# The weight sums of a seven-product stage: from VectorE to accumulating memory transfers

## The chip, the cores and the metric

The kernel runs on one core of a Trainium2 chip. The metric is the device time of one execution in microseconds (us), as the median of the runs of the same program.

## The reference

Two transformer-like blocks follow one another on a sequence of 512 tokens of width 1024, in float32. The change touches only the end of the second block, where four branches are gated and merged:

```python
branch_d = jnp.einsum('nbsw,nwd->bsnd', ys, w_branch)
g = jax.nn.sigmoid(gates.reshape(bsz, s, N_BRANCH, d))
merged = jnp.sum(g * branch_d, axis=2)
return x + merged @ w_out
```

`gates` is a product of the normalised input `h` (512 x 1024) and 4096 columns of `w_in`, so the gates are a matmul of 512 x 1024 by 1024 x 4096. `branch_d` is four products of 512 x 512 by 512 x 1024.

## The kernel before

**Splitting.** Every float32 weight is used as a sum of two reduced parts. ScalarE (ACT) copies a strip from `raw` to `w_hi` (`split_hi`, L649), VectorE (DVE) subtracts to get `w_lo` (`split_lo`, L1160), and TensorE (PE) makes three matmuls for each product: hi x hi, hi x lo, lo x hi. `w_hi` and `w_lo` have 4 places (`SPLITS`). Each engine works through the list `USED` in order; at step k, ACT and DVE make the split of step k + 3, and a split may not start before PE has finished step k - 4 of its own number (`unit_used`).

**Loading.** SP's queue loads the units of `ORDER` into `raw`, a ring of 5 strips of 512 KB (128 partitions x 1024 float32). It waits until the unit that had the place before has been split (`lo_made`).

**The seven-product stage.** The gate weights come as panels `ga`: `ga[2j]` and `ga[2j+1]` are the panels of the two branches of pair j. For pairs 2 to 15 (14 pairs) the 2 x 2 blocks of tokens and weights are multiplied by a scheme of seven instead of eight block products. The steps of one pair in `USED` are `sa`, `sb`, `br`, `sc`, `sd`: `sa` uses panel a as it is, `sb` uses two sums of weights held in the tile `s12`, `br` is the branch product, `sc` uses panel b with its left half replaced by a sum, and `sd` uses the right half of panel a after a sum has been put there. The token sums (`t_full`, `t3_full`, made by `make_tokens`) are made once, ahead of the stage. The parts are gathered in PSUM, copied and added (`gate_a`, `gate_b`), put through a sigmoid and multiplied by the branch products (`gate_pair`).

**The sums of weights before.** VectorE makes them in `combine` (L1172, L1173 for `sb`; L1176 for `sc`; L1181 for `sd`), each once per pair on 128 x 512 float32, one step before the split that needs them, and ACT's split waits for `combined`.

**GpSimd's queue.** POOL has no work between 487 us and the end of the stage: its next instruction is the reload of the kept `x2` (L620), issued when the `sb` step of the last pair has been used, and then the load of `final_row` (L623).

Of the kernel before, what the change touches and what calls it, by code (L numbers as in the profile page):

```python
# [6 lines left out]
P = 128  # L7
# [9 lines left out]
RING = 5  # L17
SPLITS = 4
AHEAD = SPLITS - 1
# [30 lines left out]
UNIT = {u: n for n, u in enumerate(ORDER)}  # L50
# [3 lines left out]
FIRST_PAIR, LAST_PAIR = 2, 2 * KT - 1  # L54
USED = []
# [5 lines left out]
HALF = S // 2  # L61
# [12 lines left out]
STEP = {u: k for k, u in enumerate(USED)}  # L74
# [158 lines left out]
def program(nc, dram, out):  # L233
    f32, f32r, bf16, i32 = mybir.dt.float32, mybir.dt.float32r, mybir.dt.bfloat16, mybir.dt.int32
    ALU, ACT, AX = mybir.AluOpType, mybir.ActivationFunctionType, mybir.AxisListType
    with ExitStack() as ctx:
# [163 lines left out]
        def sem(name):  # L400
            return ctx.enter_context(nc.semaphore(name))
# [35 lines left out]
        tiles_made, f_heads_made = sem("tiles_made"), sem("f_heads_made")  # L437

        x2_saved, x2_here = sem("x2_saved"), sem("x2_here")
        t_step, t_hi_made, combined = sem("t_step"), sem("t_hi_made"), sem("combined")  # L440
        part_made, part_kept, part_added = sem("part_made"), sem("part_kept"), sem("part_added")
        sig_made, gated = sem("sig_made"), sem("gated")
        x2_rstd, x2_norm_made, x2T_made, h2_hi_made, h2_made = (
# [44 lines left out]
        def raw_of(unit):  # L488
            return raw[:, UNIT[unit] % RING, :]
# [14 lines left out]
        def banks_of(p):  # L504

            return side if p % 2 == 0 else acc
# [50 lines left out]
        def _(pool):  # L557
# [54 lines left out]
            for t in range(1, TT):  # L612
                pool.wait_ge(relu_used, 4 * t)
                diagonal = score[:, t - 1, t * P:(t + 1) * P]
                nc.gpsimd.affine_select(out=diagonal, in_=diagonal, compare_op=ALU.is_ge, fill=OUTSIDE, base=0,
                                        pattern=[[-1, P]], channel_multiplier=1).then_inc(cut_made, 1)
            pool.wait_ge(unit_used, STEP["sb", LAST_PAIR] + 1)
            pool.wait_ge(x2_saved, 16)
            for half in (slice(0, S), slice(S, D)):
# [6 lines left out]
        def _(act):  # L626
# [8 lines left out]
            def split_hi(k):  # L635

                kind, j = USED[k]
                if kind == "sb":
                    act.wait_ge(combined, 3 * (j - FIRST_PAIR) + 1)
                elif kind == "sc":  # L640
                    act.wait_ge(combined, 3 * (j - FIRST_PAIR) + 2)
                elif kind == "sd":
                    act.wait_ge(combined, 3 * (j - FIRST_PAIR) + 3)
                else:
                    n = UNIT["ga", 2 * j] if kind == "sa" else UNIT[kind, j]
                    act.wait_ge(raw_in[n % RING], 16 * (n // RING + 1))
                if k >= SPLITS and (kind, j) != ("bs", 0):
                    act.wait_ge(unit_used, k - SPLITS + 1)
                nc.scalar.activation(split_at(k)[0][:, 0:WIDTH.get(kind, U)], strip_of(k), ACT.Copy).then_inc(hi_made, 1)  # L649
# [199 lines left out]
            for k, (kind, j) in enumerate(USED):  # L849
# [159 lines left out]
                if (kind, j) in (("dq", 2), ("dq", 3)):  # L1009
                    n = j - 1  # L1010
# [19 lines left out]
                    nc.scalar.activation(gate_b[:, :], banks_of(j)[0][:, 0:HALF], ACT.Copy).then_inc(part_kept, 1)  # L1030
                if kind == "sc":
                    act.wait_ge(gated, 2 * p)
                    nc.scalar.activation(sig[:, 1, 0:HALF], banks_of(j)[0][:, 0:HALF], ACT.Sigmoid).then_inc(sig_made, 1)
                    act.wait_ge(part_added, 3 * p + 2)
                    nc.scalar.activation(sig[:, 1, HALF:], gate_b[:, :], ACT.Sigmoid).then_inc(sig_made, 1)
                if kind == "sd":
                    act.wait_ge(part_added, 3 * p + 1)
                    act.wait_ge(part_added, 3 * p + 3)
# [29 lines left out]
        def _(dve):  # L1068
            done = [0]

            def then(ins):

                done[0] += 1
                ins.then_inc(dve_chain, 1)
                dve.wait_ge(dve_chain, done[0])
# [84 lines left out]
                nc.vector.tensor_tensor(out=lo[:, 0:width], in0=strip_of(k), in1=hi[:, 0:width].bitcast(f32),  # L1160
                                        op=ALU.subtract).then_inc(lo_made, 1)

            def combine(k):

                kind, j = USED[k] if k < len(USED) else (None, 0)
                if kind not in ("sb", "sc", "sd"):
                    return
                a, b, n = raw_of(("ga", 2 * j)), raw_of(("ga", 2 * j + 1)), j - FIRST_PAIR + 1
                if kind == "sb":
                    for u in (("ga", 2 * j), ("ga", 2 * j + 1)):  # L1170
                        dve.wait_ge(raw_in[UNIT[u] % RING], 16 * (UNIT[u] // RING + 1))
                    then(nc.vector.tensor_tensor(out=s12[:, 0, :], in0=b[:, 0:512], in1=b[:, 512:1024], op=ALU.add))  # L1172
                    nc.vector.tensor_tensor(out=s12[:, 1, :], in0=s12[:, 0, :], in1=a[:, 0:512], op=ALU.subtract)\  # L1173
                        .then_inc(combined, 1)
                if kind == "sc":
                    nc.vector.tensor_tensor(out=b[:, 0:512], in0=a[:, 0:512], in1=b[:, 0:512], op=ALU.subtract)\  # L1176
                        .then_inc(combined, 1)
                if kind == "sd":
                    dve.wait_ge(combined, 3 * (n - 1) + 1)
                    dve.wait_ge(lo_made, STEP["sa", j] + 1)  # L1180
                    nc.vector.tensor_tensor(out=a[:, 512:1024], in0=a[:, 512:1024], in1=s12[:, 1, :], op=ALU.subtract)\  # L1181
                        .then_inc(combined, 1)

            def difference(dst, part, hi, lo, hi_less, lo_less):

                then(nc.vector.tensor_tensor(out=dst, in0=hi, in1=hi_less, op=ALU.subtract))
                then(nc.vector.tensor_tensor(out=part, in0=lo, in1=lo_less, op=ALU.subtract))
                nc.vector.tensor_tensor(out=dst, in0=dst, in1=part, op=ALU.add).then_inc(t_step, 1)

            def make_tokens(kind, j):  # L1190

                hi = {(r, c): quarter(hT_hi, r, c).bitcast(f32) for r in (0, 1) for c in (0, 1)}
                lo = {(r, c): quarter(hT_lo, r, c).bitcast(f32) for r in (0, 1) for c in (0, 1)}
                full, rest = {n: t[:, :, :] for n, t in t_full.items()}, {n: t[:, :, :] for n, t in t_rest.items()}
                if (kind, j) == ("dq", 1):
                    dve.wait_ge(x2_saved, 16)
                    difference(full[1], rest[1], hi[0, 1], lo[0, 1], hi[0, 0], lo[0, 0])
                if (kind, j) == ("dq", 2):
                    dve.wait_ge(t_step, T_STEP[1, "full"])
                    then(nc.vector.tensor_tensor(out=full[2], in0=hi[1, 1], in1=full[1], op=ALU.subtract))  # L1200
                    nc.vector.tensor_tensor(out=full[2], in0=full[2], in1=lo[1, 1], op=ALU.add).then_inc(t_step, 1)
                if (kind, j) in (("dq", 3), ("dk", 0)):
                    n = 1 if kind == "dq" else 2
                    dve.wait_ge(t_step, T_STEP[2, "full"])
                    dve.wait_ge(t_hi_made, n)
                    nc.vector.tensor_tensor(out=t_lo[n][:, :, :], in0=full[n], in1=t_hi[n][:, :, :].bitcast(f32),
                                            op=ALU.subtract).then_inc(t_step, 1)
                if (kind, j) == ("ga", 1):
                    difference(t3_full[:, :, :], t3_part[:, :, :], hi[1, 1], lo[1, 1], hi[0, 1], lo[0, 1])
                if (kind, j) == ("ga", 2):  # L1210
                    dve.wait_ge(t_step, T_STEP[2, "lo"])
                    difference(full[4], rest[4], hi[1, 0], lo[1, 0],
                               t_hi[2][:, :, :].bitcast(f32), t_lo[2][:, :, :].bitcast(f32))
                if (kind, j) == ("ga", 3):
                    dve.wait_ge(t_step, T_STEP[4, "full"])
                    dve.wait_ge(t_hi_made, 3)
                    nc.vector.tensor_tensor(out=t_lo[4][:, :, :], in0=full[4], in1=t_hi[4][:, :, :].bitcast(f32),
                                            op=ALU.subtract).then_inc(t_step, 1)
                if (kind, j) == ("br", 1):
                    dve.wait_ge(t_step, T_STEP[3, "full"])  # L1220
                    dve.wait_ge(t_hi_made, 4)
                    nc.vector.tensor_tensor(out=quarter(hT_lo, 0, 1), in0=t3_full[:, :, :],
                                            in1=quarter(hT_hi, 0, 1).bitcast(f32), op=ALU.subtract).then_inc(t_step, 1)
# [303 lines left out]
            for k, (kind, j) in enumerate(USED):  # L1527
                if k + 1 < KT:
                    modulate(k + 1)
                    if k + 2 < KT:  # L1530
                        if k:
                            sum_modulation(k + 2, 0)
                        sum_modulation(k + 2, 1)
                    lower_h(k + 1)
                    for later_k in to_split(k):
                        split_lo(later_k)
                elif (kind, j) not in (("wo", 14), ("wo", 15)):
                    combine(k + AHEAD + 1)
                    for later_k in to_split(k):
                        split_lo(later_k)  # L1540
                n = HEAD_AT.get((kind, j))
# [862 lines left out]
```

## Time and profile before

| | |
|---|---|
| median of 3 runs | 1111.63 us (1111.48 to 1111.64) |
| span of the profiled execution | 1109.4 us |
| PE busy | 1100.7 us, 99% |
| DVE busy | 744.2 us, 67% |
| ACT busy | 506.9 us, 46% |
| POOL busy | 19.8 us, 2% |

The span runs from the first to the last instruction of one profiled execution. That execution has no device time of its own on record; the median of the three runs is 2.2 us above its span. Busy shares are averages over stages with different limits, and a matmul's end is modelled, so a busy PE is read by the distance between matmul starts rather than by the share.

### The profile page before, as it was taken

To read this page: it belongs to the slowest core of one execution; us is meant where nothing else is said; L and a number is where in the kernel's file an instruction comes from. 1 tells how busy PE (TensorE), PEld (TensorE's weight loads), DVE (VectorE), ACT (ScalarE), POOL (GpSimd) and SP (SyncE) were. 2 spreads that over 40 slices of the span, in tenths; PEclk is the share of its full clock that TensorE was granted. 3 is DMA by queue.
4 is the path that set the end of the run, shared out by engine and by line. 5 is a ranking of instruction groups with operands and counts; after the bars stand their busy time and mean duration, and the time that the engine had idled before them with its cause. 6 is when DMAs were issued, how large, how long until landed. Compare 5 with 4: busy or idle time off the path is not lost.

```text
span 1109.4 us, 18066 instructions
## 1 busy us (share of the span) xinstructions
PE 1100.7 (99%) x7344; PEld 931.1 (84%) x7344; DVE 744.2 (67%) x1195; ACT 506.9 (46%) x851; POOL 19.8 (2%) x40
## 2 busy tenths in 40 slices
PE   9999999999999999999999999999999999999997
PEld 8888888888888888878888887887789999999986
DVE  6875876864686247448789896447568677667853
ACT  7562354324675225533342434336544444444543
POOL 1000000000001001000000000000000000000000
PEclk9999999999999999999999999999999999999999
DMA  9543324432215433522223232231121322333241
GB/s 372 220 149 125 125 68 133 127 102 73 74 58 167 139 95 111 185 74 79 77 76 95 77 95 68 66 114 58 58 73 61 114 93 80 115 115 114 81 186 76
DMA packets 33618, 121.09 MB, mean 109 GB/s; under 512 B 3824, under 2 KB 3824, under 8 KB 33536
## 3 DMA queue, kind: packets, MB, share of 16 engines
q1 hardware_dynamic: 30672, 109.88, 29.7%
q0 software_dynamic: 2720, 10.03, 2.7%
q8 instruction: 58, 0.95, 0.4%
q14 instruction: 24, 0.20, 0.1%
q10 hardware_dynamic: 144, 0.03, 0.0%
HBM read 115.74 MB, written 4.19 MB: 108 GB/s over the span
## 4 chain that ended last, share of the span: by engine, by line
PE 98%; DMA 1%; DVE 1%; ACT 0%; SPq 0%; issue 0%; ACTq 0%
PE acc L1829 22%; PE acc L1831 21%; PE acc L1830 21%; PE acc L1841 2%; PE side L1841 2%; PE acc L1839 2%; PE side L1839 2%; PE acc L1837 2%; PE side L1837 2%; PE acc L2189 2%; PE side L1829 2%; PE side L1830 2%; PE side L1831 2%; PE side L2071 2%; PE side L1984 2%; PE side L2189 1%
## 5 line engine op out<-in xcount | busy, mean ns | idle before, releaser
L1160 DVE TENSOR_TENSOR w_lo<-raw,w_hi 128x1024 fp32r<-128x1024 f32 (+2 forms) x194 | 225.8, 1165 | 149.7 <-ACT w_hi L649 146.8
L1829 PE MATMUL acc<-hT_hi,w_hi 128*128 128x512 f32 x648 | 258.9, 400 | 0.0
L1831 PE MATMUL acc<-hT_hi,w_lo 128*128 128x512 f32 x648 | 252.8, 390 | 0.0
L1830 PE MATMUL acc<-hT_lo,w_hi 128*128 128x512 f32 x648 | 252.4, 390 | 0.0
L649 ACT ACTIVATE w_hi<-raw 128x1024 fp32r<-128x1024 f32 (+2 forms) x194 | 195.6, 1009 | 115.4 <-PE acc L1831 87.7
L1829 PEld LDWEIGHTS acc<-hT_hi,w_hi 128*128 128x128 f32 x648 | 121.9, 188 | 26.9 <-issue 2.9
L1831 PEld LDWEIGHTS acc<-hT_hi,w_lo 128*128 128x128 f32 x648 | 121.6, 188 | 26.1
L1830 PEld LDWEIGHTS acc<-hT_lo,w_hi 128*128 128x128 f32 x648 | 121.9, 188 | 23.6
L1829 PE MATMUL acc<-w_hi,hT_hi 128*128 128x512 f32 (+1 forms) x152 | 60.3, 396 | 0.0
L1831 PE MATMUL acc<-w_hi,hT_lo 128*128 128x512 f32 (+1 forms) x152 | 58.8, 387 | 0.0
L1830 PE MATMUL acc<-w_lo,hT_hi 128*128 128x512 f32 (+1 forms) x152 | 58.7, 386 | 0.0
L1160 DVE TENSOR_TENSOR w_lo<-s,w_hi 128x1024 fp32r<-128x1024 f32 x14 | 17.2, 1225 | 39.8 <-ACT w_hi L649 39.8
L912 ACT ACTIVATE silu_e<-acc 128x512 f32<-128x512 f32 x32 | 19.0, 594 | 53.8 <-PE acc L1831 53.8
L1829 PEld LDWEIGHTS acc<-w_hi,hT_hi 128*128 128x128 f32 x152 | 28.5, 188 | 6.3 <-issue 1.0
L1831 PEld LDWEIGHTS acc<-w_hi,hT_lo 128*128 128x128 f32 x152 | 28.5, 188 | 5.6
L1830 PEld LDWEIGHTS acc<-w_lo,hT_hi 128*128 128x128 f32 x152 | 28.6, 188 | 5.4 <-issue 0.2
L789 ACT ACTIVATE probs<-side,small 128x128 f32<-128x128 f32 (+3 forms) x32 | 16.9, 529 | 34.3 <-DVE small L1448 25.1
L1841 PE MATMUL side<-hT_hi,w_lo 128*128 128x256 f32 x112 | 31.7, 283 | 0.0
L1841 PE MATMUL acc<-hT_hi,w_lo 128*128 128x256 f32 x112 | 31.7, 283 | 0.0
L1839 PE MATMUL side<-hT_lo,w_hi 128*128 128x256 f32 x112 | 31.7, 283 | 0.0
L1839 PE MATMUL acc<-hT_lo,w_hi 128*128 128x256 f32 x112 | 31.7, 283 | 0.0
L1837 PE MATMUL acc<-hT_hi,w_hi 128*128 128x256 f32 x112 | 31.7, 283 | 0.0
(461 smaller groups left out, 2251.5 us busy)
## 6 DMA issues: line engine op xcount, KB each, us to landing
raw<-in_ga SPq DMA_DIRECT2D x32, 512.0 KB, 4.5
ada_raw<-in_ada SPq DMA_DIRECT2D x16, 512.0 KB, 11.5
raw<-in_wo SPq DMA_DIRECT2D x16, 512.0 KB, 3.5
raw<-in_br SPq DMA_DIRECT2D x16, 512.0 KB, 3.5
raw<-in_q SPq DMA_DIRECT2D x8, 512.0 KB, 3.5
raw<-in_u SPq DMA_DIRECT2D x8, 512.0 KB, 4.0
raw<-in_gp SPq DMA_DIRECT2D x8, 512.0 KB, 4.5
raw<-in_ada_w SPq DMA_DIRECT2D x8, 512.0 KB, 3.6
```

The costliest lines, as they stand in the source:

```text
L649: nc.scalar.activation(split_at(k)[0][:, 0:WIDTH.get(kind, U)], strip_of(k), ACT.Copy).then_inc(hi_made, 1)
L912: nc.scalar.activation(gate_e(gates), acc[RESULT[kind, j] % 4][:, :], ACT.Exp, scale=-1.0)\
L1160: nc.vector.tensor_tensor(out=lo[:, 0:width], in0=strip_of(k), in1=hi[:, 0:width].bitcast(f32), op=ALU.subtract).then_inc(lo_made, 1)
L1829: nc.tensor.matmul(ps, w[0], x[0], start=first, stop=False)
L1830: nc.tensor.matmul(ps, w[0], x[1], start=False, stop=False)
L1831: return nc.tensor.matmul(ps, w[1], x[0], start=False, stop=last)
L1837: nc.tensor.matmul(out_, w[0][:, cols], x[0][:, kt, :], start=first and kt == 0, stop=False, skip_group_check=not first)
L1839: nc.tensor.matmul(out_, w[0][:, cols], x[1][:, kt, :], start=False, stop=False, skip_group_check=not first)
L1841: ins = nc.tensor.matmul(out_, w[1][:, cols], x[0][:, kt, :], start=False, stop=kt == 3, skip_group_check=not first)
L1984: ins = nc.tensor.matmul(ps[p0:p0 + B, n0:n0 + width], k[:, tok], right, start=True, stop=True)
L2071: ins = nc.tensor.matmul(side[3][:, h * P:(h + 1) * P], v, probsT[:, s % 2, b * P:(b + 1) * P], start=(b == 0), stop=(b == blocks - 1))
L2189: return nc.tensor.matmul((acc + side)[h][:, :], w[:, h * P:(h + 1) * P], x[:, j, :], start=start and j == 0, stop=stop and j == KT - 1)
```

## The change

The four VectorE sums of each pair go. In their place POOL's queue issues five DMA transfers for each pair, four of which accumulate (they add to what the destination holds): the first puts the left half of b into both halves of `s12`, the second adds the right half of b to both, the third adds the left half of a to the left half of b in `raw`, the fourth adds the left half of a to the second half of `s12`, and the fifth adds the second half of `s12` to the right half of a in `raw`. ACT's splits wait for the transfers' semaphores. The transfers only add, so the scheme is one with only plus signs among the weights: the token sums change sign accordingly, and the sigmoids of the second gate read their input with scale -1.

```diff
+            pool.wait_ge(t_step, T_STEP[3, "full"])
+            for j in range(FIRST_PAIR, LAST_PAIR + 1):
+                ga, summed_here = dram["ga"], 64 * (j - FIRST_PAIR)
+                a, b = raw_of(("ga", 2 * j)), raw_of(("ga", 2 * j + 1))
+                twice = [ga[2 * j + 1, :, n:n + 512].unsqueeze(1).broadcast_to([P, 2, 512]) for n in (0, 512)]
+                if j > FIRST_PAIR:
+                    pool.wait_ge(lo_made, STEP["sb", j - 1] + 1)
+                    pool.wait_ge(s12_sum, summed_here)
+                pool.dma_start(s12[:, :, :], twice[0]).then_inc(s12_sum, 16)
+                pool.wait_ge(s12_sum, summed_here + 16)
+                pool.dma_start(s12[:, :, :], twice[1], accum_op=ALU.add).then_inc(s12_sum, 16)
+                n = UNIT["ga", 2 * j + 1]
+                pool.wait_ge(raw_in[n % RING], 16 * (n // RING + 1))
+                if j > FIRST_PAIR:
+                    pool.wait_ge(b_sum, 16 * (j - FIRST_PAIR))
+                pool.dma_start(b[:, 0:512], ga[2 * j, :, 0:512], accum_op=ALU.add).then_inc(b_sum, 16)
+                pool.wait_ge(s12_sum, summed_here + 32)
+                pool.dma_start(s12[:, 1, :], ga[2 * j, :, 0:512], accum_op=ALU.add).then_inc(s12_sum, 16)
+                pool.wait_ge(s12_sum, summed_here + 48)
+                pool.wait_ge(lo_made, STEP["sa", j] + 1)
+                pool.dma_start(a[:, 512:1024], s12[:, 1, :], accum_op=ALU.add).then_inc(s12_sum, 16)
             pool.wait_ge(unit_used, STEP["sb", LAST_PAIR] + 1)
...
                 if kind == "sb":
-                    act.wait_ge(combined, 3 * (j - FIRST_PAIR) + 1)
+                    act.wait_ge(s12_sum, 64 * (j - FIRST_PAIR) + 48)
                 elif kind == "sc":
-                    act.wait_ge(combined, 3 * (j - FIRST_PAIR) + 2)
+                    act.wait_ge(b_sum, 16 * (j - FIRST_PAIR) + 16)
                 elif kind == "sd":
-                    act.wait_ge(combined, 3 * (j - FIRST_PAIR) + 3)
+                    act.wait_ge(s12_sum, 64 * (j - FIRST_PAIR) + 64)
...
-                    nc.scalar.activation(sig[:, 1, 0:HALF], banks_of(j)[0][:, 0:HALF], ACT.Sigmoid).then_inc(sig_made, 1)
+                    nc.scalar.activation(sig[:, 1, 0:HALF], banks_of(j)[0][:, 0:HALF], ACT.Sigmoid, scale=-1.0).then_inc(sig_made, 1)
                     act.wait_ge(part_added, 3 * p + 2)
-                    nc.scalar.activation(sig[:, 1, HALF:], gate_b[:, :], ACT.Sigmoid).then_inc(sig_made, 1)
+                    nc.scalar.activation(sig[:, 1, HALF:], gate_b[:, :], ACT.Sigmoid, scale=-1.0).then_inc(sig_made, 1)
...
-            def combine(k):
...
-                if kind == "sb":
-                    for u in (("ga", 2 * j), ("ga", 2 * j + 1)):
-                        dve.wait_ge(raw_in[UNIT[u] % RING], 16 * (UNIT[u] // RING + 1))
-                    then(nc.vector.tensor_tensor(out=s12[:, 0, :], in0=b[:, 0:512], in1=b[:, 512:1024], op=ALU.add))
-                    nc.vector.tensor_tensor(out=s12[:, 1, :], in0=s12[:, 0, :], in1=a[:, 0:512], op=ALU.subtract)\
-                        .then_inc(combined, 1)
-                if kind == "sc":
-                    nc.vector.tensor_tensor(out=b[:, 0:512], in0=a[:, 0:512], in1=b[:, 0:512], op=ALU.subtract)\
-                        .then_inc(combined, 1)
-                if kind == "sd":
-                    dve.wait_ge(combined, 3 * (n - 1) + 1)
-                    dve.wait_ge(lo_made, STEP["sa", j] + 1)
-                    nc.vector.tensor_tensor(out=a[:, 512:1024], in0=a[:, 512:1024], in1=s12[:, 1, :], op=ALU.subtract)\
-                        .then_inc(combined, 1)
...
-                    combine(k + AHEAD + 1)
```

In `make_tokens` the first difference swaps its operands, and the second and fourth token sums get one `scalar_tensor_tensor` each (with the factor -1) in place of a `tensor_tensor`; the number of instructions stays the same.

## Rows read from the trace of the kernel before

**Rows 1.** Stages: us, each engine's busy time, granted PE clock, DMA share, GB/s.
```profile
core 0: us, PE busy (x) PEld busy (x) DVE busy (x) ACT busy (x) POOL busy (x), PEclk, DMA share, GB/s
...
857.10:1042.00 184.90, 184.90 (x1283) 173.11 (x1283) 133.93 (x185) 80.84 (x130) 0.00 (x0) 1.00 0.29 102
...
1100.00:1109.40 9.40, 3.45 (x16) 2.52 (x14) 3.45 (x5) 4.67 (x12) 0.00 (x0) 0.93 0.55 223
```

**Rows 2.** Lines L1837 and L1172: durations min/median/max, first and last start.
```profile
L1837 PE MATMUL acc<-t_hi,w_hi x84: 277/283/283, 860.0 to 1057.6; 128*128 128x256 f32 x84
...
L1172 DVE TENSOR_TENSOR s<-raw x14: 679/682/693, 831.4 to 1035.7; 128x512 f32<-128x512 f32 x14
```

**Rows 3.** Timeline of one pair: start us, duration us, engine, line, operation [idle before].
```profile
917.88 1.23 DVE L1160 TENSOR_TENSOR w_lo<-s,w_hi 128x1024 fp32r<-128x1024 f32 x1 [3.06 <-ACT w_hi L649]
...
932.09 0.28 PE L1837 MATMUL acc<-t_hi,w_hi 128*128 128x256 f32 x1
932.21 0.28 PE L1839 MATMUL acc<-t_lo,w_hi 128*128 128x256 f32 x1
...
932.35 1.06 ACT L649 ACTIVATE w_hi<-s 128x1024 fp32r<-128x1024 f32 x1 [2.42 <-PE side L1831]
...
933.45 1.23 DVE L1160 TENSOR_TENSOR w_lo<-s,w_hi 128x1024 fp32r<-128x1024 f32 x1 [3.06 <-ACT w_hi L649]
...
937.85 0.28 PE L1837 MATMUL side<-t_hi,w_hi 128*128 128x256 f32 x1
```

**Rows 4.** The same pair, branch matmuls: two successive starts.
```profile
931.64 0.39 PE L1830 MATMUL side<-yd_lo,w_hi 128*128 128x512 f32 x1
931.87 0.39 PE L1831 MATMUL side<-yd_hi,w_lo 128*128 128x512 f32 x1
```

**Rows 5.** DVE's timeline after the split of `s12`, same pair.
```profile
934.59 0.69 DVE L1176 TENSOR_TENSOR raw<-raw 128x512 f32<-128x512 f32 x1
935.40 1.23 DVE L1160 TENSOR_TENSOR w_lo<-raw,w_hi 128x1024 fp32r<-128x1024 f32 x1
936.54 0.42 DVE L1241 TENSOR_TENSOR gate_a<-acc,gate_a 128x256 f32<-128x256 f32 x1
936.88 0.68 DVE L1248 TENSOR_TENSOR merged_part<-side,sig 128x512 f32<-128x512 f32 x1
937.59 0.69 DVE L1252 TENSOR_TENSOR m_full<-m_full,merged_part 128x512 f32<-128x512 f32 x1
938.32 0.69 DVE L1248 TENSOR_TENSOR merged_part<-acc,sig 128x512 f32<-128x512 f32 x1
```

**Rows 6.** DMA issues by tile: count, KB each, median us from issue to landing.
```profile
raw<-in_wo SPq DMA_DIRECT2D x16, 512.0 KB, 3.5
...
x_kept<-x POOLq DMA_DIRECT2D x1, 2048.0 KB, 8.5
...
raw<-in_pw SPq DMA_DIRECT2D x4, 256.0 KB, 2.6
...
gate_row<-in_gate_b POOLq DMA_DIRECT2D x1, 512.0 KB, 4.4
...
final_row<-in_final_g POOLq DMA_DIRECT2D x1, 512.0 KB, 7.4
...
kv_row<-in_kv_g POOLq DMA_DIRECT2D x1, 64.0 KB, 5.6
```

**Rows 7.** DMA queues over the span: packets, MB, share of 16 engines.
```profile
q1 hardware_dynamic: 30672, 109.88, 29.7%
q0 software_dynamic: 2720, 10.03, 2.7%
```

**Rows 8.** DMA issues in one pair, 925.7 to 941.4 us.
```profile
raw<-in_ga SPq DMA_DIRECT2D x2, 512.0 KB, 6.3
raw<-in_br SPq DMA_DIRECT2D x1, 512.0 KB, 4.3
```

**Rows 9.** Timeline of the start and the end of the stage, DVE and ACT.
```profile
826.98 1.23 DVE L1188 TENSOR_TENSOR t_full<-t_full,t_part 128x1024 f32<-128x1024 f32 x1
...
832.88 1.06 ACT L649 ACTIVATE w_hi<-s 128x1024 fp32r<-128x1024 f32 x1 [1.35 <-DVE s L1173]
...
1041.27 1.06 ACT L649 ACTIVATE w_hi<-s 128x1024 fp32r<-128x1024 f32 x1 [2.42 <-PE side L1831]
```

**Rows 10.** POOL's queue: issues of DMAs, and the wait before them.
```profile
338.05 0.56 POOL L593 DMA_DIRECT2D gate_row<-in_gate_b  x1 [233.12 <-PE acc L1831]
...
1050.11 1.53 POOL L620 DMA_DIRECT2D x<-x_kept  x2 [562.73 <-PE acc L1841]
```

More of the change, by code:

```diff
@@ L439, in program @@
         x2_saved, x2_here = sem("x2_saved"), sem("x2_here")
-        t_step, t_hi_made, combined = sem("t_step"), sem("t_hi_made"), sem("combined")
+        t_step, t_hi_made = sem("t_step"), sem("t_hi_made")
+        s12_sum, b_sum = sem("s12_sum"), sem("b_sum")
         part_made, part_kept, part_added = sem("part_made"), sem("part_kept"), sem("part_added")
@@ L1161, in split_lo @@
                                         op=ALU.subtract).then_inc(lo_made, 1)
-            def combine(k):
[L1165 to L1168, printed above, removed]
-                if kind == "sb":
-                    for u in (("ga", 2 * j), ("ga", 2 * j + 1)):
-                        dve.wait_ge(raw_in[UNIT[u] % RING], 16 * (UNIT[u] // RING + 1))
-                    then(nc.vector.tensor_tensor(out=s12[:, 0, :], in0=b[:, 0:512], in1=b[:, 512:1024], op=ALU.add))
-                    nc.vector.tensor_tensor(out=s12[:, 1, :], in0=s12[:, 0, :], in1=a[:, 0:512], op=ALU.subtract)\
-                        .then_inc(combined, 1)
-                if kind == "sc":
-                    nc.vector.tensor_tensor(out=b[:, 0:512], in0=a[:, 0:512], in1=b[:, 0:512], op=ALU.subtract)\
-                        .then_inc(combined, 1)
-                if kind == "sd":
-                    dve.wait_ge(combined, 3 * (n - 1) + 1)
-                    dve.wait_ge(lo_made, STEP["sa", j] + 1)
-                    nc.vector.tensor_tensor(out=a[:, 512:1024], in0=a[:, 512:1024], in1=s12[:, 1, :], op=ALU.subtract)\
-                        .then_inc(combined, 1)
             def difference(dst, part, hi, lo, hi_less, lo_less):
@@ L1196, in make_tokens @@
                     dve.wait_ge(x2_saved, 16)
-                    difference(full[1], rest[1], hi[0, 1], lo[0, 1], hi[0, 0], lo[0, 0])
+                    difference(full[1], rest[1], hi[0, 0], lo[0, 0], hi[0, 1], lo[0, 1])
                 if (kind, j) == ("dq", 2):
                     dve.wait_ge(t_step, T_STEP[1, "full"])
-                    then(nc.vector.tensor_tensor(out=full[2], in0=hi[1, 1], in1=full[1], op=ALU.subtract))
-                    nc.vector.tensor_tensor(out=full[2], in0=full[2], in1=lo[1, 1], op=ALU.add).then_inc(t_step, 1)
+                    then(nc.vector.scalar_tensor_tensor(out=full[2], in0=hi[1, 1], scalar=-1.0, in1=full[1],
+                                                        op0=ALU.mult, op1=ALU.subtract))
+                    nc.vector.tensor_tensor(out=full[2], in0=full[2], in1=lo[1, 1], op=ALU.subtract).then_inc(t_step, 1)
                 if (kind, j) in (("dq", 3), ("dk", 0)):
@@ L1211, in make_tokens @@
                     dve.wait_ge(t_step, T_STEP[2, "lo"])
-                    difference(full[4], rest[4], hi[1, 0], lo[1, 0],
-                               t_hi[2][:, :, :].bitcast(f32), t_lo[2][:, :, :].bitcast(f32))
+                    then(nc.vector.tensor_tensor(out=full[4], in0=hi[1, 0], in1=t_hi[2][:, :, :].bitcast(f32), op=ALU.add))
+                    then(nc.vector.tensor_tensor(out=rest[4], in0=lo[1, 0], in1=t_lo[2][:, :, :].bitcast(f32), op=ALU.add))
+                    nc.vector.scalar_tensor_tensor(out=full[4], in0=full[4], scalar=-1.0, in1=rest[4],
+                                                   op0=ALU.mult, op1=ALU.subtract).then_inc(t_step, 1)
                 if (kind, j) == ("ga", 3):
```

## The prediction

> **What bounds the kernel now.** I read the page's engine table first: PE is busy 99% of the span, so something must make PE wait, or must make its work shorter, before the time moves. The change leaves the matmuls as they are. Then I read the stages. In the seven-product stage PE shows no idle time, at full granted clock, while DVE is busy 133.9 of 184.9 us and the DMA engines 29% [rows 1]. The sums recur 14 times between 831.4 and 1035.7 us, so a pair takes 204.3 / 13 = 15.7 us [rows 2]. PE's own work for a pair is 84 matmuls of 256 columns, which start 0.12 us apart [rows 3], and 24 of 512 columns, 0.23 us apart [rows 4]: 10.1 + 5.5 = 15.6 us. So PE is the bound of a pair to within 0.1 us, and all that DVE, ACT and the DMAs do must fit into 15.7 us.
>
> Next I read one pair's timeline for the slack of the step that gets its weights latest from the sums, `sb`. ACT may split `s12` at 932.35, when PE has ended `br` of the pair before; DVE's part ends at 933.45 + 1.23 = 934.68; PE starts `sb` at 937.85 [rows 3]. The slack is 3.2 us.
>
> **What is taken away.** Four DVE sums per pair of 0.69 us, 2.8 us of DVE time [rows 2, 5]. DVE is not the bound, and PE has 0.1 us to recover in a pair, so this is worth at most 14 x 0.1 = 1.4 us, and I count it as 0. ACT's waits for these sums go too, but PE has never waited for them. The token sums keep their number and size; the sign of the sigmoid's scale is a parameter of the same instruction: 0.
>
> **What is added.** Five transfers per pair on POOL's queue. I call them D1 to D5 in order of issue. POOL waits for D1 before it issues D2, for D2 before D4, for D4 before D5, and before the next D1 for D5 and for the split of `s12` (`lo_made` of `sb`). That is a ring: the four transfers D1, D2, D4, D5 follow one another, each from issue to landing, and the next pair can't start them earlier since there is one `s12`. No double buffer lets two pairs overlap. D3 is issued while D2 runs and has `b_sum` of its own; it is needed only two steps later. SP's queue and its waits are unchanged, and behind the waiting instructions on POOL stand only the reload of `x2` and `final_row`, which wait for PE's last `sb` anyway [rows 10]. Behind ACT's wait for D4 stand the sigmoids of the pair before and the split of the next `br`, behind these DVE's gating, and for the gating PE's next `br` waits.
>
> The budgets, from the rows of before: from the end of the split of one `s12` (917.88 + 1.23 = 919.11) to the start of ACT's split of the next (932.35) are 13.2 us, and 16.4 us with the slack [rows 3]. D1 + D2 + D4 have to fit in there. And D1 + D2 + D4 + D5 have to fit in 15.7 us, or the ring gets longer than PE's pair and every pair pays the difference.
>
> **The price of one transfer.** The trace has no accumulating DMA and no DMA from POOL in this stage. Rates first: 30672 packets of queue 1 carried 109.88 MB in 29.7% of 16 x 1109.4 us, or 20.8 GB/s for each engine, 333 GB/s for all; queue 0, POOL's, comes to the same [rows 7]. So 512 KB take 1.6 us and 256 KB 0.8 us of moving. POOL's lightly loaded transfers then leave a fixed part: `gate_row` 4.4 - 1.6 = 2.8 us; the store of 2048 KB 8.5 - 6.3 = 2.2 us [rows 6]. I take 2.5. SP's queue is shorter, 3.5 us for 512 KB and 2.6 for 256 KB [rows 6]; these are the lower bound. POOL's under load were 7.4 us for 512 KB and 5.6 for 64 KB [rows 6]; these are the upper bound for a plain one.
>
> An accumulating transfer must also read its destination. From below this costs nothing more, if that read runs beside the other; from above I allow that it doubles the whole transfer, fixed part included, if destination reads are not overlapped. I take the middle that follows from the rate: the bytes that are read count twice.
>
> - D1, 512 KB, plain: 2.5 + 1.6 = 4.1 us.
> - D2, 512 KB, accumulating: 2.5 + 3.1 = 5.6 us, and 0.8 us because D3's 256 KB go through the same engines at that time: 6.4.
> - D4 and D5, 256 KB, accumulating: 2.5 + 1.6 = 4.1 us each.
> - POOL's wake-up and issue between them, 0.1 us each: 0.4 us. An issue itself keeps POOL 0.56 us, which lies in the landing times [rows 10].
> - SP's three loads of 512 KB per pair come in one burst, and in this stage they take 4.3 and 6.3 us against 3.5 alone [rows 6, 8]. One or another member of the ring meets this burst: 0.8 us.
>
> The ring: 4.1 + 6.4 + 4.1 + 4.1 + 0.4 + 0.8 = 19.9 us, say 20.0, against 15.7. Below, with nothing for accumulating and nothing for company: 4.1 + 4.1 + 3.3 + 3.3 + 0.4 = 15.2, and 12.2 with SP's durations. Above: 4.1 + 8.2 + 6.6 + 6.6 + 2.0 = 27.5.
>
> **The sum.** D1 of the first pair waits for the third token sum, which ends at 826.98 + 1.23 = 828.2 [rows 9]. D4 lands 4.1 + 6.4 + 4.1 + 0.3 = 14.9 us later, at 843.1, ten us after ACT's first split of `s12` before (832.88). PE notices only part of that. D4 of the last pair lands 13 rings later, 843.1 + 260 = 1103.1. Before, this split started at 1041.3 and could have started 3.2 us later without PE's noticing, at 1044.5 [rows 3, 9]. The delay at PE is 58.6 us. Add the gating: after the split of `s12` starts, DVE needs until 938.32 + 0.69 - 933.45 = 5.6 us from the start of its own part to end the second product, less the removed sum (0.7), so 1.1 + 4.9 = 6.0 us after ACT's start [rows 3, 5]; I allow 0.4 for ACT's share of it. PE, which starts `sb` 2.3 us after ACT's start and needs 24 x 0.12 = 2.9, wants to begin `br` 5.2 us after it: 1.2 us more for the last pair. For the others this lies within the ring's surplus. After the last pair all is as before, since SP's loads for the last product and the reload of `x2` shift along. Together 60 us. The span would be 1109.4 + 60 = 1169.4 us, and with the 2.2 us by which the median stands above the span, 1171.6: I say 1172 us.
>
> In each pair PE then stands still for about 20.0 - 15.6 = 4.4 us, in one or two pieces, before `sb` and before `br`.
>
> **Rivals.**
>
> *The transfers stay hidden (no change).* What decides is the point at which D1 + D2 + D4 + D5 with their gaps pass 15.7 us. If accumulating costs nothing and the fixed part is as small as SP's, the ring is 12.2 us; with POOL's fixed part and nothing else 15.2. Either gives PE its weights in time, as D1 + D2 + D4 are then 9.6 or 11.8 us against 13.2. The time would be 1111.6, less up to 1.4 us for PE's last tenth. For it speaks that rates on both queues are alike [rows 7]; against it speak the slower rows of POOL's queue, the company of D3 and of SP's burst (with these 1.6 us the ring is 16.8 and the time 1128), and that the destination has to be read. The Trainium skill's page "DMA: Bandwidth & Descriptors", section "Anatomy of one DMA — SWDGE (gpsimd) path", gives a transfer from this queue as about 2.0 us plus its bytes at 436 GB/s; an estimate from that page is 3.2 + 3.2 + 2.6 + 2.6 = 11.6 us, and by it the change would cost nothing. The trace disagrees with it so far as `gate_row` goes, 4.4 us against 3.2. Chance of this rival: 0.12, of which 0.02 fall to a gain above 0.2%.
>
> *Accumulating is much slower than moving.* At twice the whole duration the ring is 27.5 us, D4 of the last pair lands at 828.2 + 20.0 + 357.5 = 1205.7, the delay is 162 us, and the time 1274. No row speaks against it, as none accumulates. Chance 0.13 for a ring beyond 24 us.
>
> *TensorE's clock falls in the pauses.* In the stage it is granted in full; at the end of the kernel, where PE works 3.45 of 9.4 us, the mean is 0.93 [rows 1]. Were half of each pair's matmuls to run at 1.2 GHz, PE's pair would take 15.6 + 7.8 = 23.4 us plus the 1.2 of gating, which passes the ring by 4.6 us: 13 x 4.6 = 60 us more, 1232. Pauses of some 4 us are short and much of the slowing would use up surplus of the ring. Chance 0.08.
>
> *My forecast,* a ring of 16 to 24 us with the clock kept: 0.67. Its own range is 16.8 us (1128) to 24 us: 828.2 + 18 + 13 x 24 = 1158, less 1044.5, plus 1.2, or 1226.
>
> **The range.** From the forecast's own 1128 to 1226 (0.67), down to take in the edge where the ring barely passes the pair, up to the clock's case and the lighter part of slow accumulation: 1118 to 1255. Left out are about 0.11 below and 0.08 above.
>
> **Chances.** A measurement of this kernel tells some 0.2% (2.2 us) from no change. Faster 0.02, within 0.2% 0.10, slower 0.88.
>
> **What would show each step.** In the profile after: POOL's issues of D1 recur every 20 us instead of PE's 15.7, with D5's landing as the releaser, not DVE's `lo_made`. ACT's split of `s12` waits for a DMA and not for PE. PE has an idle piece before the matmuls on `t_hi` in each pair, released by `w_lo`. D1's landing is near 4.1 us, D2's 6, D4's and D5's 4. DVE's busy time is 14 x 2.8 = 39 us less. The forecast is wrong if the durations of the accumulating transfers lie outside these, if the start shows that pairs can run ahead of one another, or if PE's clock in the stage is under 1.00.

## The result, and the profile after

The changed kernel takes 1204.49 us (median of 3 runs, 1204.13 to 1205.54) against 1111.63: ratio 1.0838, 95% interval 1.0818 to 1.0857. It is slower by 92.9 us; 60 were forecast. The profiled execution has a span of 1203.8 us, 94.4 more than before. Of all executions quoted here one stands apart and is in no median: the fourth of experiment 3 took 1364.06 us at a mean granted clock of 0.753, the other three 1140 to 1142 us at 0.994 to 0.995.

The page of the kernel after: engines (busy us, share of the span, instructions), and from its list of groups the two that name the loss (busy us, mean ns, then idle time before them and its releaser).

```profile
PE 1130.3 (94%) x7342; PEld 952.0 (79%) x7344; DVE 710.6 (59%) x1139; ACT 503.6 (42%) x851; POOL 83.5 (7%) x110
...
L671 ACT ACTIVATE w_hi<-s 128x1024 fp32r<-128x1024 f32 x14 | 14.8, 1056 | 125.7 <-DMA s<-in_ga 125.7
...
L1840 PE MATMUL acc<-t_hi,w_hi 128*128 128x256 f32 x84 | 30.8, 367 | 31.4 <-DVE w_lo L1182 21.6
```

ACT's split of `s12` now waits for a transfer in each of the 14 pairs, where in 13 of them it waited for PE before [rows 3, 9]. And PE waits, at the first matmul of `sb`. Its waits in the stage, by line (total us, times, longest), from the weight loads that stand ahead of the matmuls:

```profile
PEld acc L1840 <- DVE w_lo L1182: 23.0, 7, 4.4
PEld side L1840 <- DVE w_lo L1182: 20.9, 8, 5.2
PEld side L1840 <- ACT gate_a L1045: 14.6, 7, 2.3
PEld acc L1840 <- ACT gate_a L1045: 11.8, 7, 2.3
```

Before, PE waited for nobody in the stage. The first two rows are the wait for the split of `s12`, 43.9 us or 3.1 in the mean of the 14 pairs. The last two are a second pause within `sb`, 26.4 us or 1.9 in the mean, up to 2.3: the second half of `sb` goes into a bank that ACT must have copied (`gate_a`), and ACT gets to that copy only after two more splits and three sigmoids.

One ring on POOL's queue (start, time of the issue, idle before it and releaser). L626 is D1, L628 D2, L633 D3, L635 D4, L638 D5:

```profile
935.86 0.75 POOL L626 DMA_DIRECT2D s<-in_ga  x1 [3.00 <-DVE w_lo L1182]
940.26 1.19 POOL L628 DMA_DIRECT2D s<-in_ga  x1 [3.65 <-DMA s<-in_ga]
941.00 1.36 POOL L633 DMA_DIRECT2D raw<-in_ga  x1
950.12 0.84 POOL L635 DMA_DIRECT2D s<-in_ga  x1 [7.76 <-DMA s<-in_ga]
954.36 0.84 POOL L638 DMA_DIRECT2D raw<-s  x1 [3.40 <-DMA s<-in_ga]
958.19 0.75 POOL L626 DMA_DIRECT2D s<-in_ga  x1 [2.99 <-DVE w_lo L1182]
```

From D1 to D1 are 22.3 us: 4.4 to D2, 9.9 to D4, 4.2 to D5, 3.8 to the next D1. The label of the last row calls `w_lo` the releaser, but that split (below) had ended at 956.42; D5, issued at 954.36 and landed 3.3 us later, at 957.7, came last.

The durations from issue to landing over all 14 pairs (min, median, max), D1, D2, D4 and D5 in this order:

```profile
DMA to landing us min/median/max: 3.9/4.1/4.1
...
DMA to landing us min/median/max: 5.8/9.5/10.3
...
DMA to landing us min/median/max: 4.0/4.0/7.6
...
DMA to landing us min/median/max: 3.3/3.3/3.3
```

D2 is the long one, and its spread says that it is not long by nature: the first pair's took 5.8. What else runs in that ring is on SP's, ACT's, DVE's and PE's timelines:

```profile
940.81 0.33 SPq L549 DMA_DIRECT2D raw<-in_br  x1
941.18 0.91 SPq L549 DMA_DIRECT2D raw<-in_ga  x2
...
954.10 1.06 ACT L671 ACTIVATE w_hi<-s 128x1024 fp32r<-128x1024 f32 x1 [9.86 <-DMA s<-in_ga]
...
955.19 1.23 DVE L1182 TENSOR_TENSOR w_lo<-s,w_hi 128x1024 fp32r<-128x1024 f32 x1 [10.49 <-ACT w_hi L671]
...
956.47 0.39 PE L1840 MATMUL acc<-t_hi,w_hi 128*128 128x256 f32 x1 [4.15 <-DVE w_lo L1182]
...
957.47 0.41 PE L1840 MATMUL acc<-t_hi,w_hi 128*128 128x256 f32 x1
957.68 0.41 PE L1842 MATMUL acc<-t_lo,w_hi 128*128 128x256 f32 x1
...
960.28 0.58 PE L1840 MATMUL acc<-t_hi,w_hi 128*128 128x256 f32 x1 [1.33 <-ACT gate_a L1045]
```

SP's three loads of 512 KB are issued 0.6 to 1.8 us after D2. From the third ring on the first of them comes between 0.4 us before and 0.7 us after D2's issue, since these loads too wait for the last pair's splits. In the second ring it came 3.3 us after D2, and there D4 took the 7.6 us and D2 only 6.0. In the pair shown, the matmuls of `sb` start 0.21 us apart from 956.9 us on, and not 0.12 as before [rows 3]. Over the stage the DMA engines are busy 62%, and PE's clock is no longer granted in full (PE, PEld, DVE, ACT, POOL busy, clock, DMA share, GB/s):

```profile
842.00:1120.00 278.00, 217.20 (x1337) 197.47 (x1336) 113.80 (x146) 86.06 (x140) 56.10 (x62) 0.90 0.62 150
```

### The profile page after: what moved, and what is told of

The parts are those of the page before. It is cut to its first block, busy times and chain, and to the rows that moved or that the text cites. A ratio compares the mean times of both kernels' runs of the same rounds, so it can differ in the third digit from the quotient of the medians.

```text
span 1203.8 us, 18098 instructions
## 1 busy us (share of the span) xinstructions
PE 1130.3 (94%) x7342; PEld 952.0 (79%) x7344; DVE 710.6 (59%) x1139; ACT 503.6 (42%) x851; POOL 83.5 (7%) x110
## 4 chain that ended last, share of the span: by engine, by line
PE 73%; issue 13%; DMA 6%; POOL 3%; ACT 2%; DVE 2%; SPq 0%; POOLq 0%; ACTq 0%; DVEq 0%
PE acc L1832 19%; PE acc L1834 18%; PE acc L1833 18%; DMA s<-in_ga 5%; PE acc L2192 2%; PE side L2074 1%; PE side L1987 1%; PE side L2192 1%; DVE w_lo L1182 1%; POOL s L628 1%; ACT w_hi L671 1%; POOL raw L633 1%; PE side L2059 1%; PE side L1833 1%; PE side L1832 1%
## 5 line engine op out<-in xcount | busy, mean ns | idle before, releaser
L671 ACT ACTIVATE w_hi<-s 128x1024 fp32r<-128x1024 f32 x14 | 14.8, 1056 | 125.7 <-DMA s<-in_ga 125.7
L1840 PE MATMUL acc<-t_hi,w_hi 128*128 128x256 f32 x84 | 30.8, 367 | 31.4 <-DVE w_lo L1182 21.6
L1840 PE MATMUL side<-t_hi,w_hi 128*128 128x256 f32 x84 | 26.3, 313 | 32.3 <-DVE w_lo L1182 19.2
L1840 PEld LDWEIGHTS acc<-t_hi,w_hi 128*128 128x128 f32 x84 | 20.8, 248 | 35.1 <-DVE w_lo L1182 23.0
L1840 PEld LDWEIGHTS side<-t_hi,w_hi 128*128 128x128 f32 x84 | 17.0, 202 | 35.5 <-DVE w_lo L1182 20.6
L626 POOL DMA_DIRECT2D s<-in_ga x14 | 10.4, 744 | 380.7 <-DVE t_full L1189 341.2
```

The lines of the kernel that those rows point to most:

```text
L1840: nc.tensor.matmul(out_, w[0][:, cols], x[0][:, kt, :], start=first and kt == 0, stop=False, skip_group_check=not first)
```

## The experiments

Eleven kernels ran, each timed in several rounds beside the kernel before. All are edits of the changed kernel, except the one without sums, which is an edit of the kernel before. The rings quoted are the mean distance of D1's issues, first to last, over 13.

**1. No burst.** SP's loads from pair 3 on are cut short.

```diff
                 width = WIDTH.get(kind, U)
+                if kind == "ga" and j >= 2 * FIRST_PAIR + 2 or kind == "br" and j > FIRST_PAIR:
+                    width, src = 16, src[:, 0:16]
```

> SP's loads of the gate panels and branch strips from pair 3 on bring 16 columns in place of 1024, so the weights used there are stale; all waits and all of POOL's transfers stay. Theory A (the second transfer of the ring is long because SP's burst of three loads of 512 KB shares the DMA engines with it): its landing time falls from 9.5 us to that of the first pair, 5.8 to 6.4, the ring from 22.3 to about 19 us, the time from 1204 to about 1160 us. Theory B (accumulating from HBM is slow by itself): 9.5 us stays, and 1204 us. Theory C (the third transfer, issued beside the second, takes its share): most of the 9.5 us stays, the time falls by under 15 us.

Measured: 1161.68 us, ratio 1.0455 (1.0436 to 1.0474). Landings of D1, D2 and D4:

```profile
DMA to landing us min/median/max: 3.8/4.1/4.3
...
DMA to landing us min/median/max: 5.5/6.0/7.3
...
DMA to landing us min/median/max: 3.9/4.0/5.3
```

Only D2 is shorter, 6.0 in place of 9.5. The ring is 19.0 and not 22.2 us, and 13 x 3.2 = 41 us are what the time fell by (42.8). So the burst makes D2 long; that accumulating from HBM takes 9.5 us by itself is refuted.

**2. D3 late.** The block that issues D3 is moved behind the wait for D4.

```diff
                 pool.dma_start(s12[:, :, :], twice[1], accum_op=ALU.add).then_inc(s12_sum, 16)
+                pool.wait_ge(s12_sum, summed_here + 32)
+                pool.dma_start(s12[:, 1, :], ga[2 * j, :, 0:512], accum_op=ALU.add).then_inc(s12_sum, 16)
+                pool.wait_ge(s12_sum, summed_here + 48)
...
                 pool.dma_start(b[:, 0:512], ga[2 * j, :, 0:512], accum_op=ALU.add).then_inc(b_sum, 16)
-                pool.wait_ge(s12_sum, summed_here + 32)
-                pool.dma_start(s12[:, 1, :], ga[2 * j, :, 0:512], accum_op=ALU.add).then_inc(s12_sum, 16)
-                pool.wait_ge(s12_sum, summed_here + 48)
```

> The third transfer (256 KB into panel b) is issued after the fourth has landed, just ahead of the fifth, no more beside the second. Theory A (SP's burst makes the second long): it stays above 8 us; some 0.8 to 1.5 us less, the ring near 21.5 plus what the third takes from the fifth and first, so the time between 1190 and 1210 us. Theory C (the third transfer makes it long): the second falls to about 6 us, the ring to 19, the time to about 1165 us, unless the third lengthens the fifth and first by as much.

Measured: 1218.12 us, ratio 1.0956 (1.0940 to 1.0973), slower than the change itself and 8 us above the upper end of what was expected. Landings of D2 and D5:

```profile
DMA to landing us min/median/max: 5.6/8.3/9.0
...
DMA to landing us min/median/max: 4.7/4.8/6.2
```

D2 gains 1.2 us and D5 loses 1.5, since now D3 goes beside it. The 1.2 us are not the price of D3's company alone, for the burst has moved as well: its first load now comes 1.2 to 1.6 us before D2 in most pairs, where it came some 0.5 us after it. Without a burst D3 costs D2 little: the first pair has none in either kernel, and D2 takes 5.6 us here and 5.8 with D3 beside it. POOL must also issue D3 (0.55 us to the next issue) between D4 and D5, where before this lay under D2. The ring is 23.1. As a time, D3 had stood in the cheaper place.

**3. Plain copies.** The four accumulating transfers lose `accum_op=ALU.add`; D2's line is shown, and D3, D4 and D5 change likewise.

```diff
-                pool.dma_start(s12[:, :, :], twice[1], accum_op=ALU.add).then_inc(s12_sum, 16)
+                pool.dma_start(s12[:, :, :], twice[1]).then_inc(s12_sum, 16)
...
```

> All five transfers of a pair are plain copies of the same sizes, none accumulates, so the sums of weights are not made. If the read of the destination is a real load (my sum counted it as bytes read twice: 1.6 us in the second, 0.8 in the fourth and fifth), the ring falls by about 3 us or more, since the third also moves less: 1155 to 1170 us. Theory B (accumulating is slow by itself): the second falls from 9.5 to about 4.5 us, the ring to about 16, and the time to 1120 to 1130 us. If accumulating costs nothing: 1204 us as after.

Measured: 1141.57 us, ratio 1.0267 (1.0249 to 1.0284); ring 17.4 us. The time lies between the two ranges expected, and so confirms neither. Landings of D1, D2, D4 and D5:

```profile
DMA to landing us min/median/max: 3.9/4.0/4.5
...
DMA to landing us min/median/max: 3.8/4.0/6.3
...
DMA to landing us min/median/max: 2.9/5.8/6.4
...
DMA to landing us min/median/max: 2.3/2.3/4.8
```

Here the fastest ones are free of company. Against the fastest accumulating ones, adding costs D2 1.6 to 1.8 us (5.6 with D3 out of the way, 5.8 with it, against 4.0), D4 1.1 (4.0 against 2.9) and D5 1.0 (3.3 against 2.3). The burst has moved: it starts 1.2 to 1.7 us after D2 in most pairs and meets D4, whose median is 2.9 us above its fastest. The ring is shorter by 4.8 us; 1.7 + 1.1 + 1.0 = 3.8 of it is the three additions, the rest less company.

**4. Burst late.** SP's loads of a pair's two panels wait for D4 of the pair before; the load of the branch strip is not held back.

```diff
                 width = WIDTH.get(kind, U)
+                if kind == "ga" and j % 2 == 0 and j // 2 >= FIRST_PAIR + 2:
+                    sp.wait_ge(s12_sum, 64 * (j // 2 - 1 - FIRST_PAIR) + 48)
```

> SP's loads of the gate panels of pair j wait in addition for the fourth transfer of pair j - 1, so that the burst no longer meets the second transfer but the fifth and the first. Theory A (whatever transfer of the ring meets the burst gets longer by 3 to 4 us): the second falls to about 6 us, the fifth or first grow, and the time changes little, 1185 to 1215 us. Rival (it is the second alone that suffers, because it moves most bytes and has the third beside it): the ring falls to 19 to 20 us and the time to 1165 to 1180 us.

Measured: 1207.14 us, ratio 1.0860 (1.0840 to 1.0881). Landings of D2 and D5:

```profile
DMA to landing us min/median/max: 5.5/5.7/8.3
...
DMA to landing us min/median/max: 3.3/6.8/7.0
```

D2 gives back 3.8 us and D5 takes 3.5 more; the ring, 22.2 us, is what it was, and the time can't be told from the change's (1.0818 to 1.0857). So the long duration goes with the burst and does not belong to D2. The branch strip's load alone, some 1.2 us behind D1, leaves D1's median at 4.1 us; in two pairs D1 takes 5.5 and 6.1.

**5. Two tiles for the sums.** Odd pairs up to 11 use two places of `m_full` that are not in use yet, and D1 of the next pair is issued beside D4 of this one; semaphores are split accordingly.

```diff
+        s12b = at("s12b", M + 12288, [P, 2, 4 * P])
+
+        def s12_of(j):
+            return s12b if j % 2 and j <= 11 else s12
...
+                pool.dma_start(s_j[:, 1, :], ga[2 * j, :, 0:512], accum_op=ALU.add).then_inc(d45, 16)
+                early = j < LAST_PAIR and s12_of(j + 1) is not s_j
+                if early:
+                    copy_b(j + 1)
+                pool.wait_ge(d45, 32 * p + 16)
```

> Odd pairs up to 11 keep their sums in a second tile of 4 KB per partition (two places of m_full that are not yet in use), and the first transfer of the next pair is issued beside the fourth of this one. For pairs 2 to 12 the ring is then the second and the longer of fourth and first: 9.8 + 4.4 = 14.2 us, under PE's 15.6. Theory D (the time is set by the chain of waits, one transfer after another, and not by how much the DMA engines move): those pairs run at PE's pace, only pairs 13 to 15 pay 6 to 7 us each and the start some: 1130 to 1145 us. Rival E (the engines' load, 0.62 of their time in the stage, sets it): the transfers only get longer, 1185 us or more.

Measured: 1141.72 us, ratio 1.0271 (1.0254 to 1.0288). The middle of the stage:

```profile
860.00:1020.00 160.00, 156.04 (x1078) 145.43 (x1077) 88.45 (x115) 66.90 (x109) 42.89 (x47) 1.00 0.85 210
```

With the same transfers, now 85% of the DMA engines' time and 210 GB/s, PE is busy 156 of 160 us at full clock. The load on the engines is higher than in the changed kernel, and the loss is gone where two pairs overlap. So the chain of waits sets the time, not the load. Of the 30 us that are left, pairs 13 to 15, which have one tile and rings of 22.4 us, would account for some 20 (an estimate, 3 x 6.7).

**6. Two tiles up to pair 5.** The same with `j <= 5`: six rings of four transfers more.

> The kernel with two tiles for the sums, but the second is used only by pairs 3 and 5, so that the pairs from 7 on have the ring of four transfers; 6 more rings than in the run up to pair 11, which took 1141.7 us. If the loss is a fixed 22.4 - 15.6 = 6.8 us for each ring: 1141.7 + 6 x 6.8 = 1182 us, within 4. If the loss is due to the load on the DMA engines as a whole, it does not follow the number of rings: under 1165 or over 1195 us.

Measured: 1184.25 us, ratio 1.0650 (1.0634 to 1.0666). Six rings cost 42.5 us, 7.1 each, where 22.4 - 15.6 = 6.8 was expected.

**7. Only two sums by transfers.** DVE makes the two sums of `s12` again (all plus signs); D3 and D5 stay with POOL, and D1, D2 and D4 go.

```diff
+                then(nc.vector.tensor_tensor(out=s12[:, 0, :], in0=b[:, 0:512], in1=b[:, 512:1024], op=ALU.add))
+                nc.vector.tensor_tensor(out=s12[:, 1, :], in0=s12[:, 0, :], in1=a[:, 0:512], op=ALU.add)\
+                    .then_inc(s_made, 1)
```

> VectorE makes the two sums of s12 again; only the sum in panel b (third transfer) and that in panel a (fifth) are made by accumulating transfers, so no ring is left: VectorE's sums start from the loaded panels. Theory D (the chain of four dependent transfers is the whole loss): the two that remain, 4 and 3.3 us beside other traffic, are hidden, 1110.5 to 1113 us, as before; VectorE's relief of 1.4 us per pair gains nothing that can be measured. Rival (what costs is accumulating beside the splits, or POOL's issues): part of the 93 us remains, over 1120 us.

Measured: 1111.01 us, ratio 0.9995 (0.9987 to 1.0004): no change that can be told. D3 and D5 take 7.0 and 7.3 us (medians) in the company of each other and the burst, and are hidden.

**8. No sums at all,** in the kernel before: the four sums of each pair are left out, and the split of `s12` reads panel b.

```diff
...
-                    combine(k + AHEAD + 1)
...
```

> The kernel before with the four sums of each pair left out altogether, not made by anybody; ACT's splits wait for the loads instead. It is the most that relieving VectorE could give. My sum put this at 0 to 1.4 us (0.1 us of each pair's 15.7): 1110.2 to 1111.6 us. Rival (VectorE's load holds PE back somewhere in the stage): 1106 us or less.

Measured: 1111.29 us, ratio 0.9997 (0.9988 to 1.0006). Freeing DVE of all four sums is worth nothing that can be measured. Experiments 7 and 8 bound the gain that the change could have had; no version tried beats the kernel before by more than the measurement tells.

**9. Filler matmuls.** 32 matmuls of 256 columns whose result is overwritten, ahead of the wait in `sb`, in pairs 3 to 15.

```diff
                 if kind == "sb":
+                    if p:
+                        for n in range(FILL):
+                            nc.tensor.matmul(ps[2][:, 0:HALF], h[0, 0][0][:, 0, 0:P], h[0, 0][0][:, 0, :],
+                                             start=True, stop=True)
                     w = weights(k)
```

> As after, and 32 matmuls of 128 x 256 into the bank half that the step overwrites are put ahead of the wait for the split of s12 in pairs 3 to 15: 3.8 us of work in PE's pause of some 3 to 4 us, so that PE is hardly idle there. Theory D (the ring sets the pace and PE's clock falls within its surplus): the same within 3 us, 1201 to 1208 us, and the granted clock in the stage rises from 0.90 to 0.97 or more. Rival (the fallen clock costs some us in each pair): 1190 us or less.

Measured: 1194.17 us, ratio 1.0748 (1.0732 to 1.0765). Neither theory's figure: 10 us less than the change, with the clock in the stage at 0.98. Landings of D1 and D2:

```profile
DMA to landing us min/median/max: 3.5/3.7/3.9
...
DMA to landing us min/median/max: 5.6/8.7/10.1
```

The gain is in the transfers: the ring is 21.4 us, 13 x 0.85 = 11 us less in all. It isn't PE's own work that got faster and let the kernel end earlier, for the ring holds no PE work. What shortens D2 goes with the burst's timing. Where its first load comes 1.0 to 1.1 us after D2 (pairs 5, 6 and 13), D2 takes 7.7 to 7.9 us; where it comes 0.4 us after (pairs 8 and 10), 9.4 to 9.6. That the one causes the other is not tested by itself.

**10. Ten fillers** in place of 32.

> As the kernel with filler matmuls, but 10 in place of 32, 1.2 us of work, which leaves PE a pause of 2 to 3 us before the split of s12 arrives. If the gain of 10 us goes with the share of time in which PE is busy: 1199 to 1202 us. If it goes with the clock being kept or not: near 1194 us where the granted clock in the stage is 0.97 or more, near 1204 us where it is 0.90.

Measured: 1202.81 us, ratio 1.0815 (1.0789 to 1.0841), ring 22.0, D1 3.9 and D2 9.2 us, clock 0.94 in the stage. Ring, D1, D2 and clock all lie between the kernels with no filler and with 32, but the time can't be told from the change's (1.0818 to 1.0857).

**11. Fillers without the burst.**

> The kernel with 32 filler matmuls ahead of the wait for the split of s12, and at once SP's loads from pair 3 on cut to 16 columns (stale weights). Filler alone gave 1194.2 us, against 1204.5; its first transfer landed in 3.7 us and not 4.1, its second in 8.7 and not 9.5, and the burst came 0.4 to 0.5 us later against the second. If the filler's gain is a matter of when the burst comes, nothing is left of it without a burst: 1161 us, as the run without burst alone, first transfer 4.1. If busy matmuls make the transfers themselves shorter: first transfer 3.7, ring 18.6 or less, 1150 to 1156 us.

Measured: 1164.87 us, ratio 1.0478 (1.0460 to 1.0495). D1 is 3.8 us (4.1 without fillers) but the ring 18.9, 0.1 less than in experiment 1. As a time this run is inconclusive: with a ring of 19 us the fillers, 3.8 us on top of 15.6, no longer fit into PE's pause, and PE becomes the bound: it waits only 3.3 us in the whole stage, and from the last D4's issue to the end are 78.1 us, against 71.3 in experiment 1. The ring itself never waited for PE: each D1 follows D5's landing as closely as before. So it says that nearly all of the filler's 0.85 us needs the burst; the filler shifts SP's loads 0.3 to 0.4 us against D2. Why D1 lands 0.3 to 0.4 us sooner stays open, and the fillers may not be the cause: in this run the first pair's D1, ahead of any filler, took 3.7 us already.

## Why the prediction was right, and where it was off

**What bounds the kernel, and what the change could gain: right.** PE was the bound, DVE's relief was counted as 0, and experiment 8 gives the same. DVE's busy time fell by 33.6 us instead of 39, because neighbouring DVE instructions overlap by some 0.1 us and busy time counts the overlap once.

**The ring: right, and shown.** Four transfers in a chain, longer than PE's pair, each pair paying the difference. Experiment 5 removes the loss by letting two pairs overlap, with all transfers kept; experiment 6 puts the price back in proportion. The rival of hidden transfers fell: the smallest ring seen with one tile, that of plain copies, is 17.4 us, over 15.7.

**The start: right, to the tenth by luck.** D4 of the first pair was to land at 843.1; it was issued at 839.13 and took 4.0, which is 843.1. D1 was issued at 828.67 and not 828.2, and the gaps were longer by 0.3 us in all; D2, free of the burst, took 5.8 and not 6.4.

**The step that was off is the price of company in the ring's sum:** 0.8 us for D3 and 0.8 us for SP's burst, 1.6 together. Measured they are 3.9 together: D2's median is 9.5 us, against 5.6 in the one pair with neither D3 nor burst beside it (experiment 2, first pair). The burst makes nearly all of it: 3.5 us go when it is taken away (9.5 - 6.0, experiment 1), and D3 without a burst makes some 0.2 to 0.4 (5.8 to 6.0 against 5.6), half of its term or less. The burst's 1.6 MB need 4.7 us at 333 GB/s, and it seems that D2 has to share with most of it. I had read the price from how much SP's loads are lengthened by each other and thought of a chance meeting [rows 8]; but the burst is released by splits that follow from the ring's own D4, so it meets a member of the ring every time, and experiment 4 shows that shifting it only chooses the victim. The other terms, forecast and measured: D1 4.1 and 4.1; D2 alone 5.6 and 5.6; D4 4.1 and 4.0; D5 4.1 and 3.3; the gaps 0.4 and 1.4, taken from the distances of the issues (22.3) less the four landings (20.9); they are three of 0.3 and, ahead of D1, one of 0.54. The errors partly cancel: company 2.3 and gaps 1.0 too little, D5 0.8 and D4 0.1 too much, 2.4 in all. So the ring was 20.0 in the forecast and is 22.45 on the mean from the first D4 to the last (839.13 to 1130.92, over 13): 13 x 2.45 = 32 us, and 60 + 32 = 92 us of 94.4. The rest comes behind the last ring: from the landing of the last D4 to the end are 68.9 us (1134.9 to 1203.8), where the sum had 66.3.

**The cost of adding: near in size.** That the bytes read count twice was an assumption, 1.6 us for 512 KB and 0.8 for 256; measured 1.6 to 1.8 and 1.0 to 1.1 (experiment 3). Two sizes don't show that the second read is what costs the time.

**The pauses of PE: near in sum, and wrong in the second's cause.** 4.4 us were forecast for each pair, all of the ring's surplus. Measured are 5.0 in the mean (3.1 + 1.9), of a surplus of 22.4 - 15.7 = 6.7. The remaining 1.7 go, as far as the pair shown tells, into matmuls at the lower clock: some 20 of them start 0.09 us later each than before, about 2 us. For the second I had named DVE's gating ahead of `br`; it is the bank that ACT has yet to copy, ACT being late with all that stands behind its wait for D4.

**The clock: wrong, and cheap.** It was to be kept; it is 0.90 in the stage. The first matmuls after the two pauses shown take 0.39 and 0.58 us against 0.28. That the clock's fall is nearly free was argued with the ring's surplus, and holds as far as the runs go: with it kept at 0.98 (experiment 9) the gain of 10 us is matched by that of the rings, 11.

**The prediction's own signs.** It named three signs of being wrong, and two of them are met: D2 takes 9.5 us and not about 6, and the clock in the stage is under 1.00. The third is not: no pair ran ahead of another. The time of 1204 us lies within 1118 to 1255, with the main mechanism right and a term of it mis-sized.

## What to carry to other kernels

Before work is handed from an engine to DMA, count the dependent transfers of one round, each from issue to landing, and compare the sum with the round of the bounding engine: here 22 us (20 forecast) against 15.7, though the DMA engines were only 62% busy, and for the sake of 2.8 us of an engine whose work lay beside the path. A loop of transfers through one buffer is a latency chain, and here a second buffer broke it, where cheaper transfers (plain ones, ring 17.4 us) did not. Where a burst of other loads is released by the same event as the chain, put most of its moving time on the chain: here 3.5 us of 4.7, where 0.8 had been allowed.

## What the runs showed of the hardware

- An accumulating transfer costs 1.6 to 1.8 us more than a plain one at 512 KB (5.6 to 5.8 against 4.0 us) and 1.0 to 1.1 more at 256 KB (3.3 against 2.3 from SBUF, 4.0 against 2.9 from HBM). Plain ones on POOL's queue mostly land in 3.8 to 4.1 us at 512 KB, away from the burst. By the fit in the Trainium skill's page "DMA: Bandwidth & Descriptors", section "Anatomy of one DMA — SWDGE (gpsimd) path", an estimate is 3.2 and 2.6 us. The measured plain ones stand above the first and, with 2.9 and 2.3, on both sides of the second.
- Three loads of 512 KB on SP's queue, issued some 0.5 us after an accumulating transfer of 512 KB on POOL's, take it from 6.0 to 9.5 us (experiment 1 against the change).
- The issue of D2 is recorded with 1.19 us on POOL and that of D1 with 0.75; D3's issue starts 0.74 us after D2's, so the record of 1.19 us does not keep the next issue away.
- D1's median is 0.3 to 0.4 us shorter in the two runs with 32 filler matmuls (3.7 and 3.8 against 4.1 us). Not explained, and not shown to come from the fillers.
